# A transformer block on one core: the second half of the modulation summed as rows inside u's tiles, spread by transfers, with squares moved and another place for gate weights

## The reference, cut to what matters

```
mod_x = silu(c) @ w_ada + b_ada          # 6*D numbers
sh1x, sc1x, g1x, sh2x, sc2x, g2x = split(mod_x, 6)
hx = rmsnorm(x, norm1_g) * (1 + sc1x) + sh1x
q, k, v, o, gates, u, vb, ga, gb = split(hx @ w_in)
h_a = bidirectional mLSTM(q, k, v, gates)           # also over the context
y_a = rmsnorm(h_a) * sigmoid(o)
y_b = gelu(u) * (w_spatial @ rmsnorm(gelu(vb), vnorm_g) + b_spatial)
merged = sigmoid(ga) * (y_a @ w_pa) + sigmoid(gb) * (y_b @ w_pb)
xs = x + g1x * (merged @ w_out)
h2 = rmsnorm(xs, norm2_g) * (1 + sc2x) + sh2x
xs = xs + g2x * ((silu(h2 @ w_ff1) * (h2 @ w_ff3)) @ w_ff2)
out = rmsnorm(xs, final_g)
```

## Time and profile before

| | |
|---|---|
| median of 3 runs | 1833.02 us |
| the profiled execution's own time | 1837.14 us |
| its span | 1835.5 us |
| PE busy | 1778.0 us (97%) |
| DVE, ACT, POOL busy | 59%, 33%, 9% |
| mean granted TensorE clock | 0.988 |

### The profile page before, as it was taken

How to read it: one execution, slowest core, us unless ns; L and a number is a source line. 1 busy time by engine, 2 the same in 40 slices (tenths; PEclk the granted TensorE clock), 3 DMA queues, 4 the chain that set the end, 5 groups by cost and what they waited for, 6 DMA issues and landing times.

```text
span 1835.5 us, 23349 instructions
## 1 busy us (share of the span) xinstructions
PE 1778.0 (97%) x8636; PEld 1487.3 (81%) x8636; DVE 1090.8 (59%) x1706; ACT 597.5 (33%) x935; POOL 166.3 (9%) x202
## 2 busy tenths in 40 slices
PE   6899999999999999999999999999999999999997
PEld 3697988979797888788888888888888888778886
DVE  4587636465556466555432445775565656676667
ACT  6533231423222313444310213533343333312112
POOL 1002020200112000111200000000000001232210
PEclk9999999999999899999999999999999999999999
DMA  7211111202068022423733243123222232632212
GB/s 303 67 48 35 59 47 44 71 23 70 12 217 311 8 84 69 160 98 106 271 99 92 91 161 126 35 75 109 69 91 69 83 100 69 246 132 91 91 46 92
DMA packets 99730, 186.65 MB, mean 102 GB/s; under 512 B 5674, under 2 KB 74426, under 8 KB 95314
## 3 DMA queue, kind: packets, MB, share of 16 engines
q1 hardware_dynamic: 83906, 130.11, 21.0%
q0 software_dynamic: 15760, 55.68, 8.7%
HBM read 149.04 MB, written 36.73 MB: 101 GB/s over the span
## 4 chain that ended last, share of the span: by engine, by line
PE 83%; DVE 8%; DMA 4%; issue 3%; ACT 1%; DVEq 0%; SPq 0%; POOL 0%; POOLq 0%; ACTq 0%
PE PD L2065 23%; PE PD L2483 10%; PE PM L2483 10%; PE PD L2503 6%; PE PM L2503 6%; PE PD L2398 5%; PE PM L2346 4%; PE PD L2346 4%; PE PD L2081 3%; DMA ada<-in_w_ada 3%; PE PM L2417 1%; PE PD L2417 1%; PE PD L2150 1%; DVE kT L1432 1%; PE PM L2323 1%
## 5 line engine op out<-in xcount | busy, mean ns | idle before, releaser
L2065 PE MATMUL PD<-R_hi,whi 128*128 128x512 f32 x480 | 150.3, 395 | 0.0
L2065 PE MATMUL PD<-R_lo,whi 128*128 128x512 f32 x480 | 149.1, 392 | 0.0
L2065 PE MATMUL PD<-R_hi,wlo 128*128 128x512 f32 x480 | 148.9, 392 | 0.0
L841 POOL TENSOR_TENSOR w_raw<-w_raw,g2B 128x2048 f32<-128x2048 f32 x11 | 52.0, 4730 | 638.6 <-DMA w_raw<-in_w_ff 638.6
L2065 PEld LDWEIGHTS PD<-R_hi,wlo 128*128 128x128 f32 x480 | 90.7, 189 | 19.2
L2065 PEld LDWEIGHTS PD<-R_lo,whi 128*128 128x128 f32 x480 | 90.7, 189 | 19.1
L2065 PEld LDWEIGHTS PD<-R_hi,whi 128*128 128x128 f32 x480 | 89.7, 189 | 18.6 <-issue 0.7
L1858 DVE TENSOR_TENSOR ws_lo<-S,ws_hi 128x512 fp32r<-128x512 f32 x76 | 56.3, 742 | 77.2 <-ACT ws_hi L1210 77.2
L868 ACT ACTIVATE whi<-raw 128x1024 fp32r<-128x1024 f32 x56 | 56.1, 1049 | 126.7 <-PE PD L2065 124.0
L2081 PE MATMUL PD<-whi,R_hi 128*128 128x256 f32 x256 | 72.9, 285 | 0.8 <-ACT vaug L934 0.8
L2081 PE MATMUL PD<-wlo,R_hi 128*128 128x256 f32 x256 | 72.6, 283 | 0.0
(11 more groups left out here) (479 smaller groups left out, 4665.4 us busy)
## 6 DMA issues: line engine op xcount, KB each, us to landing
rawF<-in_w_ff SPq DMA_DIRECT2D x44, 512.0 KB, 5.2
ada<-in_w_ada POOLq DMA_DIRECT2D x32, 512.0 KB, 6.2
raw<-in_w_in SPq DMA_DIRECT2D x30, 512.0 KB, 5.4
f_dram<-Fo SPq DMA_DIRECT2D x11, 1024.0 KB, 4.8
w_raw<-in_w_ff SPq DMA_DIRECT2D x11, 1024.0 KB, 5.0
f_raw<-f_dram SPq DMA_DIRECT2D x11, 1024.0 KB, 6.9
ada_raw<-in_w_ada SPq DMA_DIRECT2D x8, 1024.0 KB, 19.4
rawG<-in_w_in SPq DMA_DIRECT2D x16, 512.0 KB, 5.6
```

Of the source, the lines that this page charges most:

```text
L841: nc.gpsimd.tensor_tensor(w2_raw[par], w2_raw[par], g2B[:, :].unsqueeze(1).to_broadcast([P, 2, D]), ALU.mult)\
L2065: i = mm(dst[:, e * HALF:e * HALF + width], wk[:, k, :], part, start=(k == 0 and step == 0), stop=(k == KT - 1 and step == 2))
```

## The change

The partition sums of Tacc turn from columns to rows. Tacc is split into Tr_hi (ACT, two copies of 128x2048, written over the w_ada buffers) and Tr_lo (DVE, two subtractions, written over Tacc). With a constant `pick` (ones in column q of slice q) 16 matmuls put the four sums into four rows of one PSUM region, after u's first pair of tiles and ahead of its SV products. DVE adds b_ada, loaded as rows by POOL, and POOL stores the 4x1024 rows to HBM (`mod_dram`). From there three loads spread them: sh2x and sc2x as columns, g1x and g2x over all partitions. The 32 broadcasting matmuls, DVE's two copies and the wait on them go. a2 is made just before the out projection's residuals.

The squares of V move from behind the loop of gelus into it, with PSUM as the place for what is not needed. The last one is made after the last gelu, the others each after their tile's second gelu. t_a and t_b change places, so rawG1 lies on t_a, and the load of block 1 waits for `right_ready` 4. PE's loop over u's pairs is written out.

```diff
# memory
+        pick = sb("pick", [P, 4, 4]); pick_r = sb("pick_r", [P, 4, 4], F32R)
...
+                    with ExitStack() as tmp:
+                        Tr_hi = sb("Tr_hi", [P, 4, D], F32R, tmp)
                     ada2 = [sb(f"ada2_{k}", [P, D], stack=s3) for k in range(4)]
+                    with ExitStack() as tmp:
+                        Tr_lo = sb("Tr_lo", [P, 4, D], F32R, tmp)
                     Tacc = sb("Tacc", [P, 4, D], stack=s3)
...
                         rawG.append(sb("rawG1", [P, KT, CW], stack=s11))
+                    t_a = sb("t_a", [P, KH, HALF], stack=s5)
                     t_b = sb("t_b", [P, KH, HALF], stack=s5)
-                    t_a = sb("t_a", [P, KH, HALF], stack=s5)
# SP
-            sp.wait_ge(left_ready, 6)
+            sp.wait_ge(right_ready, 4)
             gate_block(1)
# POOL
+            pool.wait_ge(tile_done, T_U)
+            pool.dma_start(mod_rows, b_ada[:, 2*D:6*D] as 4 rows).then_inc(mod_io, 16)
+            pool.wait_ge(mod_ready, 1)
+            pool.dma_start(mod_dram, mod_rows).then_inc(mod_io, 16)
             for k in range(KT):
                 pool.wait_ge(y_f32, k + 3)
...
             pool.wait_ge(yb_out, 16 * KT)
+            pool.wait_ge(mod_io, 32)
+            pool.dma_start(mod[:, 3:5, :] as "p (q k)", mod_dram[1:3, :] as "q (k p) -> p (q k)")  # 16
...
             pool.wait_ge(tile_done, T_O)
+            pool.wait_ge(mod_io, 48)
+            pool.dma_start(xn[:, LT - 1, :], mod_dram[0:1, :].to_broadcast([P, D]))  # 16
             for t in range(LT):
                 pool.dma_start(xs[:, t, :], x_t[:, t, :]).then_inc(pool_in[t], 16)
-            pool.wait_ge(g2_ready, 1)
+            pool.wait_ge(mod_io, 64)
+            pool.wait_ge(slot_free[1], T_O // 2 + 1)
+            pool.dma_start(g2B[:, :], mod_dram[3:4, :].to_broadcast([P, D]))  # 16
+            pool.wait_ge(mod_io, 80)
# ACT, in the loop over i and t, behind the gelu
+                    if i == 1:
+                        act.wait_ge(slot_free[...], ...)
+                        own.link(nc.scalar.activation(PM[:, 2 * HALF:], V[:, t, :], ACT.Square,
+                                                      accum_out=rs[:, 0, t:t + 1]))
-            for t in range(LT):
-                own.link(nc.scalar.activation(uT[0][:, :], V[:, t, :], ACT.Square, accum_out=rs[:, 0, t:t + 1]))
+            act.wait_ge(ada2_used, 4 * KT + 4)
+            for q in range(0, 4, 2):
+                nc.scalar.activation(Tr_hi[:, q:q + 2, :], Tacc[:, q:q + 2, :], ACT.Copy).then_inc(sums_hi_d, 1)
             act.wait_ge(wspT_done, 1)
# DVE
+            v.tensor_copy(pick_r[:, :, :], pick[:, :, :])    # near the start
...
-            dve.wait_ge(T_mm, 1)
-            v.tensor_tensor(mod[:, 2:6, :] ..., PM[:, 0:4 * KT], cols[:, 48:80], ALU.add).then_inc(mod_ready, 1)
-            own.link(v.scalar_tensor_tensor(out=a2 ...))
             rsqrt(LT, D)
             for t in range(LT):
                 v.tensor_scalar(V[:, t, :], V[:, t, :], rs[:, 2, t:t + 1], None, ALU.mult).then_inc(v_scaled, 1)
             ... wsp_lo
+            for q in range(0, 4, 2):
+                dve.wait_ge(sums_hi_d, q // 2 + 1)
+                v.tensor_tensor(Tr_lo[:, q:q + 2, :], Tacc[:, q:q + 2, :], Tr_hi[:, q:q + 2, :], ALU.subtract)
...
                 if pair == 0:                       # behind vn_lo of the first pair
+                    dve.wait_ge(T_mm, 1); dve.wait_ge(mod_io, 16)
+                    v.tensor_tensor(mod_rows[:, :], PM[0:4, 2 * HALF:], mod_rows[:, :], ALU.add).then_inc(mod_ready, 1)
                     own.link(v.tensor_tensor(ta, h12, h11, ALU.subtract))
...
-            dve.wait_ge(gB_mm, 2)
-            own.link(v.tensor_copy(g1B, PM[:, 0:D])); own.link(v.tensor_copy(g2B[:, :], PM[:, D:2 * D]))
+            dve.wait_ge(mod_io, 64)
+            v.scalar_tensor_tensor(out=a2 ...).then_inc(a2_ready, 1)
# PE
-            pe.wait_ge(ada2_used, 4 * KT + 4)
-            for q in range(4):
-                for k in range(KT):
-                    last = mm(PM[:, q * KT + k:q * KT + k + 1], Tacc[:, q, k * P:(k + 1) * P], one1[:, :], ...)
             ... four transposes of w_spatial
+            def mod_sums():
+                pe.wait_ge(sums_ready, 3)           # wsp_lo and both Tr_lo
+                for q in range(4):
+                    for n, part in enumerate((Tr_hi, Tr_lo)):
+                        for e in range(2):
+                            last = mm(PM[0:4, (2 + e) * HALF:(3 + e) * HALF], pick_r[:, q, :],
+                                      part[:, q, e * HALF:(e + 1) * HALF], ...)
+                last.then_inc(T_mm, 1)
             # for each pair: two tiles of u, then
+                if pair == 0:
+                    mod_sums()
             # SV of jj = 0, then of jj = 1, ahead of which
+                    if jj == 1:
+                        pe.wait_ge(mod_ready, 1)
...
-            broadcast_gate(2, 0); broadcast_gate(5, D)      # 16 matmuls each
```

More of the change, by code:

```diff
@@ L135, in build @@
     xs_dram = nc.dram_tensor("xs_dram", [P, LT, D], F32, kind="Internal").ap()
+    mod_dram = nc.dram_tensor("mod_dram", [4, D], F32, kind="Internal").ap()
     m_dram = nc.dram_tensor("m_dram", [1, 2 * HEADS * NLAT], F32, kind="Internal").ap()
@@ L154, in build @@
         gsel = sb("gsel", [P, 16])
+        pick = sb("pick", [P, 4, 4])
+        pick_r = sb("pick_r", [P, 4, 4], F32R)
         cols = sb("cols", [P, P])
@@ L457, in build @@
         wspT_done = sem("wspT_done")
-        wsp_hi_d = sem("wsp_hi_d")
-        wsp_ready = sem("wsp_ready")
+        sums_hi_d = sem("sums_hi_d")
+        sums_ready = sem("sums_ready")
         ada2_used = sem("ada2_used")
@@ L712, in _ @@
             nc.gpsimd.memset(cs4[:, :, :], 0.0).then_inc(consts, 1)
+            own.link(nc.gpsimd.memset(pick[:, :, :], 0.0))
+            for q in range(4):
+                own.link(nc.gpsimd.memset(pick[:, q, q:q + 1], 1.0))
             credits = 0
@@ L1370, in _ @@
             dve.wait_ge(gate_in, 16 * 5)
+            dve.wait_ge(pool_own, 7)
+            v.tensor_copy(pick_r[:, :, :], pick[:, :, :]).then_inc(wgz_ready, 1)
             for kind in range(2):
@@ L1647, in _ @@
                 v.tensor_scalar(V[:, t, :], V[:, t, :], rs[:, 2, t:t + 1], None, ALU.mult).then_inc(v_scaled, 1)
-            dve.wait_ge(wsp_hi_d, 1)
+            dve.wait_ge(sums_hi_d, 3)
             v.tensor_tensor(wsp_lo[:, :, :], PM[:, HALF:2 * HALF].rearrange("p (g t) -> p g t", g=4),
-                            wsp_hi[:, :, :].bitcast(F32), ALU.subtract).then_inc(wsp_ready, 1)
+                            wsp_hi[:, :, :].bitcast(F32), ALU.subtract).then_inc(sums_ready, 1)
+            dve.wait_ge(ada2_used, 4 * KT + 4)
+            for q in range(0, 4, 2):
+                dve.wait_ge(sums_hi_d, q // 2 + 1)
+                v.tensor_tensor(Tr_lo[:, q:q + 2, :], Tacc[:, q:q + 2, :], Tr_hi[:, q:q + 2, :].bitcast(F32),
+                                ALU.subtract).then_inc(sums_ready, 1)
             dve.wait_ge(small_in, 32 * HEADS + 32)
@@ L1810, in _ @@
             m_lo(KT - 1)
-            dve.wait_ge(gB_mm, 2)
+            dve.wait_ge(mod_io, 64)
             g1B = xn[:, LT - 1, :]
-            own.link(v.tensor_copy(g1B, PM[:, 0:D]))
-            own.link(v.tensor_copy(g2B[:, :], PM[:, D:2 * D]))
-            v.tensor_copy(note[:, 0:1], g2B[:, 0:1]).then_inc(g2_ready, 1)
+            v.scalar_tensor_tensor(out=a2[:, :], in0=mod[:, 4, :], scalar=1.0, in1=cols[:, 24:32],
+                                   op0=ALU.add, op1=ALU.mult).then_inc(a2_ready, 1)
             def residual(hf, t):
@@ L2305, in _ @@
             i.then_inc(wspT_done, 1)
[L2308 to L2324, removed]
+            def mod_sums():
+                pe.wait_ge(sums_ready, 3)
+                for q in range(4):
+                    for n, part in enumerate((Tr_hi, Tr_lo)):
+                        for e in range(2):
+                            last = mm(PM[0:4, (2 + e) * HALF:(3 + e) * HALF], pick_r[:, q, :],
+                                      part[:, q, e * HALF:(e + 1) * HALF], start=(q + n == 0), stop=(q + n == 4))
+                last.then_inc(T_mm, 1)
@@ new lines, in _ @@
+            for pair in range(4):
+                for jj in (2 * pair, 2 * pair + 1):
+                    pe.wait_ge(slot_free[jj % 2], T_U // 2 + pair + 1)
+                    channels(jj % 2, N_U + pair, pair % 2, jj % 2, R_hi, R_lo)
+                if pair == 0:
+                    mod_sums()
+                for jj in (2 * pair, 2 * pair + 1):
+                    b = jj % 2
+                    pe.wait_ge(vn_ready, jj + 1)
+                    pe.wait_ge(sums_ready, 1)
+                    pe.wait_ge(y_f32, jj + 1)
+                    if jj == 1:
+                        pe.wait_ge(mod_ready, 1)
+                    for c8 in range(LT):
+                        dst = PM[:, b * NLAT + c8 * P:b * NLAT + (c8 + 1) * P]
```

(4 more changed lines are left out.)

31 lines of the change are left out of this document (17 added, 14 removed).

## The result

| | before | changed |
|---|---|---|
| median, first comparison (4 runs each) | 1833.36 us (1832.39 to 1836.06) | 1818.63 us (1813.83 to 1818.99) |
| profiled execution | 1837.14 us | 1818.99 us |
| its span | 1835.5 us | 1817.3 us |
| mean granted clock | 0.988 | 0.992 |

A forecast was written before the change was run, and what follows sets the result against it. PE was taken as the bound, busy for 97% of the span. Gains of 15.2 (sums), 7.1 (gate block 0) and 1.2 us (broadcasts) make 23.5, from a median of 1833.0 to 1809.5 us; range 1806 to 1817.

The forecast's parts named there:

- The sums: Between V's last tile and the end of u's first SV: 46.6 us become 31.4, a gain of 15.2 us.
- cover at Tr_lo: Time by which DVE finishes Tr_lo before PE needs it for the 16 matmuls: 5.6 us.
- cover at `mod_ready`: Time by which DVE's add of b_ada ends before PE asks for it, halfway through SV: 1.2 us.
- Rival B: The sums' chain ends 2 to 4 us late and PE stands: 1811.5 to 1813.5 us; chance 0.10.
- Gate block 0: Block 1's weights are requested 6.1 us sooner, so block 0 loses its excess: a gain of 7.07 us.
- Rival A: Gate block 0 stays too long despite the earlier request: gain 16.4 us, 1816.6 us; chance 0.12.
- The column transfer: Load spreading sh2x and sc2x to columns in 2048 runs of 4 bytes: at most 13.4 us, costing nothing.
- Rival D: The column transfer holds POOL's queue; it outweighs the gains above 54 us, and with 60 gives 1839 us; chance 0.03.
- The broadcasts: Before the out tiles 3.57 us go, but PE then waits for a weight split: a gain of 1.2 us.
- rival C: The idle 2.3 us before the out tiles drops the clock: a loss of 1 to 2 us, 1812; chance 0.06.
- From the traced execution to the median: The whole 23.5 us gain, read from an execution of 1837.1 us, was taken off the median of 1833.0: 1809.5.

The follow-up runs named there:

- fill_idle: The changed kernel with 10 matmuls of 512 columns, results unused, put on PE just before the out tiles; 1812.83 us, ratio 0.9878.
- fill_less: The changed kernel with 4 unused matmuls just before the out tiles, which leaves PE a stand of 1.5 us; 1815.34 us, ratio 0.9899.
- start_only: The kernel before with only the change's additions at the start: pick's five memsets, its copy and the wait for it; 1834.31 us, ratio 1.0004.
- place_undone: The changed kernel with t_a and t_b in the old order and block 1's load waiting for `left_ready` 6 again; 1821.50 us, ratio 0.9927.
- after_again: The changed kernel unaltered, timed and profiled a second time; 1815.70 us, ratio 0.9894.

## Why the prediction was wrong, step by step

**The sums: right.** 15.2 us were forecast, 15.4 measured; u's pair 21.79 (forecast 21.87), 16 matmuls 3.69 (3.76), cover at Tr_lo 6.5 us (5.6), cover at `mod_ready` 1.4 us (1.2). Rival B, with PE standing behind u's second tile, did not come; with the squares put back behind the loop it comes, with 0.8 us.

**Gate block 0: right in its mechanism, a little too large.** Block 0 takes 19.15 us and lasts no longer than the others (19.04); 7.07 us forecast, 6.8 in the two traces compared, 6.0 by the other pairs. ACT did wait 1.51 us for rawG, without holding PE. Rival A is out by both experiments.

**The column transfer: right that it costs nothing.** It landed in 3.9 us (bound taken: 13.4) after an issue of 1.18 us, and nothing waited for it. This is the DMA issue (operation, count, KB each, median us from issue to landing):

```profile
mod<-mod_dram POOLq DMA_DIRECT2D x1, 8.0 KB, 3.9
```

Rival D, which needed 54 us, is out. The rule that I set against it, from the Trainium skill, page "DMA: Bandwidth & Descriptors", section "Rules for kernel authors" (one descriptor for each element of a strided last dimension), doesn't show here as a cost: the whole changed kernel has 136 packets under 512 bytes more than the kernel before (5810 against 5674), not 2048. Whether a packet of the profile is one descriptor is not shown.

**The broadcasts: wrong, and rival C right.** The forecast was a gain of 1.2 us, from "the idle stretch of 2.3 us does not lower the clock as I read it". The new wait was named and sized well (2.3 forecast, 2.6 measured). The step that failed is the reading of the clock from one row of one execution. That row has PE busy for 0.41 of 2 us; the stand that it cuts through runs from 1601.47 to 1603.59, 2.12 us, so it was near enough in length. But the same stand is followed by half clock in six of twelve profiles, and the one I read was of the other six. At the out tiles PE stood for 2.6 us, and the clock was at half behind it in five profiles of five. So 2.6 + 78.00 = 80.6 us stand against 3.57 + 76.20 = 79.8: a loss of 0.8 us, 2.0 us off. fill_idle and fill_less show the cause, for with the stretch filled or shortened the out tiles need 76.4 us again. I gave this 0.06, and the price that I gave it (a loss of 1 to 2 us) was nearly met.

**From the traced execution to the median: wrong, and the largest part (4.1 of the 9.1 us between 1809.5 and 1818.63).** The step was "that execution is 4.1 us above the median of 1833.0, so the median should be 1809.5": the whole gain was taken off a run in which there was 4.1 us less to gain from. The table shows where such an excess can lie: behind block 1 the four profiles of kernels with the old sums agree within 0.1 us, so one run exceeds another ahead of it, and there the stage that the change takes away varies by 3.9 us and the pieces of block 0 by 0.8. In start_only's execution (span 1830.9, its own time 1832.6, 1.7 below that kernel's median) the sums would give 43.36 - 31.24 = 12.1, block 0 gives 6.0 and the rest -0.5 us, in all 17.6 us, and the medians of all runs differ by 17.1. That the runs without a profile vary in the same stages is argued from their times, not seen. Over all runs 17.1 us were gained and not 23.5. Of the 6.4 missing, the traces show 2.0 at the broadcasts and 1.1 at block 0, and the means of the profiles 1.2 at the start; the 2.1 that are left are put down to the stage of the sums by this argument alone.

**The start.** V's end lies at 593.1 to 594.5 us in the four profiles that begin as before and at 593.2 to 597.2 in eight that begin as the changed kernel (mean 593.7 and 594.9). The three of these above 596.5 (the first of the changed kernel, place_undone and fill_less) have a fall of the clock in the first head, in a place where PE had not stood for 34 us; PE in the first profile, stretches as above, and then the same work in after_again:

```profile
132.00:134.00 2.00, 2.00 (x21) 1.00 1.00 293
134.00:136.00 2.00, 2.00 (x8) 0.63 0.93 251
136.00:140.00 4.00, 4.00 (x15) 0.76 0.02 6
```
```profile
132.00:134.00 2.00, 2.00 (x14) 1.00 1.02 292
134.00:136.00 2.00, 2.00 (x10) 1.00 0.36 101
136.00:140.00 4.00, 4.00 (x19) 1.00 0.00 0
```

This fall is worth 1.5 of the 3.6 us: the 2 and 72 matmuls there take 0.70 + 17.87 us and not 0.47 + 16.57. The rest is in what PE had lost before, 2.2 us at the 20 matmuls ahead of them (132.27 against 130.05), where the clock had come back later, at 0.72 and not at 1.00 between 64 and 68 us. One kernel does both, so it is chance whether a run has it; whether the changed program makes it more likely (three of eight against none of four) stays open. start_only rules out the memsets and the copy.

Against the forecast for the profiled execution itself (1813.6, measured 1819.0) the account closes: 3.6 us at the start, 2.0 for the broadcasts, 0.3 for block 0, less 0.2 at the sums and some 0.4 at the end, is 5.3 of 5.4 us.

## What to carry to other kernels

When an instruction is taken out in front of a wait, price the stand that remains with both outcomes, and look for the same stand in several profiles, not in one: here 1.5 us were free in the one profile that has such a stand, 2.12 us were free in six profiles and not in six, and 2.6 us cost another 1.6 in all five. Four matmuls of no use were enough to get that back. Before subtracting a gain read from one trace from the median of other runs, ask in which stage that trace's excess lies: if it is the stage that the change removes, the excess is not there to be gained in a typical run, so compare the forecast with what a second profile shows of that stage. Work put between an engine and a chain of transfers (u's tiles ahead of the sums) takes away both the wait and its variation (43.4 to 47.3 us before, 31.23 to 31.25 after).

## What was not expected of the hardware

- One stand of 2.12 us, in front of the same matmuls in every profile, was followed by half clock in six executions of twelve and by full clock in six.
- The clock fell to half in the first head of three of eight executions of kernels with the same start, with PE busy throughout the stretches before and during it: 17.87 to 18.02 us for the 72 matmuls that otherwise take 16.57. The Trainium skill, page "TensorE: Matmul & The Clock Gate", section "What's actually happening", has the number of slow matmuls at the start of one kernel vary from run to run. These traces vary too, but 134 us in.
- One load of 2048 runs of 4 bytes was issued in 1.18 us and landed in 3.9 us. The median of the kernel's 32 stores of 256 KB is 2.7 us.
